# A four-layer decoder trunk: sums, additions and swaps issued in another order

## The chip, the cores and the metric

The kernel runs on one core of a Trainium2 chip. The metric is the device time of one execution in microseconds (us). TensorE (PE) multiplies matrices; VectorE (DVE), ScalarE (ACT) and GpSimd (POOL) work element by element; SyncE (SP) only issues transfers here, and ACT's queue issues some as well. Each engine runs its own list of instructions in order and waits on semaphores for the others.

## The reference, cut to what matters

There are four layers on 1032 tokens of 1024 features (1024 of a prompt, and 8 single tokens). Each layer adds a normed mixer to x:

```python
for i in range(DEPTH):
    kind, j = i % N_MIXERS, i // N_MIXERS          # a, b, c, a
    hp = rms_norm(xp, norm_pre[i])
    ...
    xp = xp + rms_norm(yp, norm_post[i])

def rms_norm(x, g):
    y = xf * lax.rsqrt(jnp.mean(xf * xf, axis=-1, keepdims=True) + NORM_EPS)
    return (y * g.astype(jnp.float32)).astype(x.dtype)
```

Mixer a is a gated MLP with a layer norm and a causal product inside chunks of 128 tokens; mixer b is attention over a window of 128 with rotary positions (each query is combined with its rotated, swapped halves); mixer c is a convolution of width 4, two gates by block-diagonal products, and a linear recurrence whose decay is

```python
log_a = -LRU_C * r.astype(jnp.float32) * jax.nn.softplus(-lam.astype(jnp.float32))
```

The softplus of `lam` depends on nothing but an input of 1024 numbers. The kernel calls it the decay constants.

## The kernel before, in words

Features lie on the partitions, tokens along the free axis, in three chunks of 344. A factor of a product is split in a high and a low part, and a product is three matmuls: high by high, high by low, low by high. One output tile of 128 features (a unit) so takes 8 x 3 x 3 = 72 matmuls of 128x344, and needs a weight block of 512 KB. SP loads these blocks (`weights(u)`, L422) into a ring of three; ACT makes the high part (`w_high`, L992), DVE the low part (`w_lo`, L1434), each for unit u while PE works on an earlier one. PE's second and first PSUM slots hold the result of a unit, and `evac` says that a slot is read.

A norm's mean of squares is a sum over partitions, made on PE by a product with `ones`. For the norm behind a mixer, `post(L, c)` (L605, L606) adds up for chunk c what DVE has summed in `ssq` and what ACT has squared last in `rx`. For the norm ahead of the next mixer, `square_sum` (L648) sums the squares of four feature tiles at a time, ACT copies the result (`copy_sums`, L1029), and `spread_sum` (L655) sums and spreads the copy to all partitions. The roots are taken on ACT as the exponential of a logarithm (L1017, L1019), `root_post` and `root_pre`.

At a border of two layers the order is written out by hand. PE runs `last_triple`: the last three output units of the old layer (j = 0, 1, 2), cut in nine pieces of one chunk each, with `post` for chunks 0 and 1 in between:

```python
TRIPLE = ((0, 0), (1, 0), (2, 0), (0, 1), (0, 2), (1, 1), (2, 1), (1, 2), (2, 2))
```

Then comes `first_pair` (L634): the first two units of the new layer, chunk by chunk. In chunk 0, all eight feature tiles of unit 0 and then of unit 1; in chunks 1 and 2, both units tile by tile. `post(prev, 2)` stands behind tile 3 of chunk 0, `spread_sum(c - 1)` behind tile 2 of chunk c. Meanwhile `cross` on ACT and on DVE turns the old result into the new x and the new operand. On ACT `out_squares` squares (L1008) and copies (L1010) each piece, and `tiles` makes the high part of x times gain (L1043) and the square (L1048). On DVE `out_add` adds the first half's part of the piece (layers a), `out_sum` adds a square to `ssq` (L1452), `tiles` multiplies two accumulator tiles by the root (L1473), makes the new x (L1476) and the low part (L1459), and `first_reads` (L1493) takes the results of the first two units out of PSUM. `next_weight(j)` copies the weights of the new layer's unit j. In a layer a three tiles of x are lent to other data (`A_EARLY`), and are fetched back per chunk by a DMA on ACT's queue (`x_own`, L1012).

In layer b the rotary combination needs each of eight query tiles with its quarters swapped. That is four DMAs a tile (L1228, `q_swap`), issued from ACT's queue when DVE has read the unit. In layer c the decay constants are a chain of 26 small DVE operations (L1918 to L1940) behind the sixth convolution tile.

At the start SP loads the first weight, pieces of x for chunk 0 and the second weight; ACT issues six small loads, loads its table and copies the first weight.

Of the kernel before, what the change touches and what calls it, by code (L numbers as in the profile page):

```python
# [17 lines left out]
ALU = mybir.AluOpType  # L18
# [67 lines left out]
def build(nc, io):  # L86
    with ExitStack() as ctx:
# [40 lines left out]
        zero = keep("zero", [P, 8])  # L128
# [18 lines left out]
        w_hi_done, w_lo_done = sem("w_hi_done"), sem("w_lo_done")  # L147
        result = sem("result")
# [15 lines left out]
        for i, kind in enumerate("abca"):  # L164
# [98 lines left out]
            if kind == "c":  # L263
# [35 lines left out]
                L.sp = at(n + "sp", o, [P, 6, KT]); o += 192  # L299
# [116 lines left out]
        def _(sp):  # L416
# [8 lines left out]
            weights(0)  # L425

# [4 lines left out]
            x_load(0, 0)  # L431
# [4 lines left out]
            for c in (1, 2):  # L436
                for g in range(X_PARTS[c]):
                    x_load(c, g)

# [25 lines left out]

            u = 2
# [76 lines left out]
        def _(pe):  # L543
# [64 lines left out]
            def last_triple(L, hi, lo):  # L608
# [10 lines left out]
                for j, c in TRIPLE:  # L619
# [3 lines left out]
                    if (j, c) == (2, 1):  # L623
                        post(L, 1)

            def first_pair(L, prev):
# [30 lines left out]
                pe.wait_ge(w_lo_done, u + 1)  # L657
                for c in range(CH):
# [3 lines left out]
                    if c == 0:  # L662
                        for k in range(KT):
                            pe.wait_ge(*L.hi_done.at(k + 1))
                            mm = products(0, k, 0)
# [3 lines left out]
                            if k == 3 and prev is not None:  # L669
                                post(prev, 2)  # L670
# [3 lines left out]
                        mm.then_inc(result, 1)  # L674
                    else:
                        for k in range(KT):
# [6 lines left out]
                            if k == 2:  # L683
                                spread_sum(c - 1)
# [295 lines left out]
        def _(act):  # L980
            act.dma_start(g_pre[:], io["g_pre"]).then_inc(gains, 16)
            act.dma_start(ident[:, :], io["ident"]).then_inc(consts, 16)
            act.dma_start(g_post[:], io["g_post"]).then_inc(consts, 16)
            act.dma_start(ln_g[:], io["ln_g"]).then_inc(consts, 16)
            act.dma_start(ln_b[:], io["ln_b"]).then_inc(consts, 16)
            act.dma_start(cvec[:], io["cvec"]).then_inc(consts, 16)
# [7 lines left out]
            def cross(prev, L):  # L994

                def out_squares(j, c):

                    slot = triple_slot(j)
                    if prev.kind == "a":
                        act.wait_ge(*prev.acc_done.at(LAST + TRIPLE.index((j, c)) + 1))  # L1000
# [10 lines left out]
                    elif j == 2:  # L1011
                        act.dma_start(x[:, 2:2 + A_EARLY, part(c)], prev.saved.rearrange("k p n -> p k n")[:, 2:2 + A_EARLY, part(c)]  # L1012
                                      ).then_inc(x_own[c], 16)
# [208 lines left out]
            def layer_b(L):  # L1222
# [20 lines left out]
                def unit_end(j):  # L1243
# [934 lines left out]
```

## Time and profile before

| what | value |
|---|---|
| time, median of three runs | 2393.58 us (2392.2 to 2395.04) |
| profiled execution | 2394.26 us, its span 2392.1 us |
| PE busy | 2320.3 us, 97% of the span, 15487 matmuls |
| DVE, ACT, POOL busy | 52%, 37%, 4% |
| high part of a weight block on ACT (L992) | 182 of 1.05 us |
| low part of a weight block on DVE (L1434) | 182 of 1.25 us |
| chain of work that ended last | PE 82%, DVE 9%, ACT 3% |

The span is the stretch from the first to the last instruction of the profile; the execution around it is 2.2 us longer. PE's 2320 us of work are one stream, and the rest of the span is the holes in it, the first 7.6 us ahead of its first matmul, and the last 15 us behind its last one. A wait is printed in brackets: how long the engine had been idle, and which instruction released it. The granted clock of a stretch is a share of 2.4 GHz.

### The profile page before, as it was taken

To read this page: it belongs to the slowest core of one execution; us is meant where nothing else is said; L and a number is where in the kernel's file an instruction comes from. 1 tells how busy PE (TensorE), PEld (TensorE's weight loads), DVE (VectorE), ACT (ScalarE), POOL (GpSimd) and SP (SyncE) were. 2 spreads that over 40 slices of the span, in tenths; PEclk is the share of its full clock that TensorE was granted. 3 is DMA by queue.
4 is the path that set the end of the run, shared out by engine and by line. 5 is a ranking of instruction groups with operands and counts; after the bars stand their busy time and mean duration, and the time that the engine had idled before them with its cause. 6 is when DMAs were issued, how large, how long until landed. Compare 5 with 4: busy or idle time off the path is not lost.

```text
span 2392.1 us, 36016 instructions
## 1 busy us (share of the span) xinstructions
PE 2320.3 (97%) x15487; PEld 2236.2 (93%) x15487; DVE 1232.4 (52%) x1759; ACT 889.1 (37%) x1280; POOL 90.7 (4%) x44
## 2 busy tenths in 40 slices
PE   8999999999999899998999999999999999999997
PEld 7999999999999798877989999979999999999996
DVE  4444445454433756667267888274444544545235
ACT  5323332332332534556352366363223332333221
POOL 0000000000000002222000010000000000000000
PEclk9999999999999999999999999999999999999998
DMA  4111111111121331111322111322111111111213
GB/s 137 45 45 45 45 45 38 43 45 45 36 98 45 127 111 54 45 45 37 107 83 70 45 45 45 118 84 77 45 54 36 45 45 38 43 45 45 89 46 107
DMA packets 58494, 145.86 MB, mean 61 GB/s; under 512 B 8904, under 2 KB 29528, under 8 KB 58328
## 3 DMA queue, kind: packets, MB, share of 16 engines
q1 hardware_dynamic: 53056, 135.34, 17.5%
q10 hardware_dynamic: 5280, 8.22, 1.3%
q8 instruction: 122, 2.00, 0.4%
q14 instruction: 36, 0.29, 0.0%
HBM read 121.47 MB, written 18.37 MB: 58 GB/s over the span
## 4 chain that ended last, share of the span: by engine, by line
PE 82%; DVE 9%; ACT 3%; DVEq 3%; ACTq 1%; issue 1%; DMA 1%; SPq 0%
PE ps L552 62%; PE ps L576 7%; PE ps L798 4%; PE ps L710 2%; PE ps L634 2%; DVE x L1476 1%; DVE l_acc L1473 1%; PE ps L816 1%; DVE w_lo L1434 1%; PE ps L855 1%; PE ps L844 1%; PE ps L703 1%; DVE l_sc L1773 1%; ACT l_h_hi L1043 1%; DVE l_hs L1988 1%
## 5 line engine op out<-in xcount | busy, mean ns | idle before, releaser
L552 PE MATMUL ps<-l_h_hi,w_hi 128*128 128x344 f32 x2448 | 527.1, 324 | 5.6 <-DVE w_lo L1434 5.6
L552 PE MATMUL ps<-l_h_lo,w_hi 128*128 128x344 f32 x2448 | 520.4, 321 | 0.0
L552 PE MATMUL ps<-l_h_hi,w_lo 128*128 128x344 f32 x2448 | 516.6, 319 | 0.0
L552 PEld LDWEIGHTS ps<-l_h_hi,w_hi 128*128 128x128 f32 x2448 | 409.2, 188 | 10.1 <-DVE w_lo L1434 6.8
L552 PEld LDWEIGHTS ps<-l_h_lo,w_hi 128*128 128x128 f32 x2448 | 414.7, 189 | 0.0
L552 PEld LDWEIGHTS ps<-l_h_hi,w_lo 128*128 128x128 f32 x2448 | 408.2, 188 | 0.0
L1434 DVE TENSOR_TENSOR w_lo<-w_raw,w_hi 128x1024 fp32r<-128x1024 f32 x182 | 227.7, 1252 | 250.3 <-ACT w_hi L992 240.2
L992 ACT ACTIVATE w_hi<-w_raw 128x1024 fp32r<-128x1024 f32 x182 | 190.8, 1049 | 109.9 <-DMA w_raw<-in_wu 78.9
L1551 DVE TENSOR_TENSOR l_tmp<-ps,rx 128x1032 f32<-128x1032 f32 x64 | 78.9, 1233 | 285.5 <-PE ps L552 285.3
L552 PE MATMUL ps<-l_y_lo,w_hi 128*128 128x344 f32 x816 | 173.1, 320 | 0.0
L552 PE MATMUL ps<-l_y_hi,w_hi 128*128 128x344 f32 x726 | 154.7, 321 | 0.8 <-DVEq L2002 0.8
L552 PE MATMUL ps<-l_y_hi,w_lo 128*128 128x344 f32 x726 | 153.1, 319 | 0.0
L1137 ACT ACTIVATE l_tmp<-l_tmp 128x1032 f32<-128x1032 f32 x32 | 34.2, 1067 | 303.9 <-DVEq L1592 303.9
L552 PEld LDWEIGHTS ps<-l_y_lo,w_hi 128*128 128x128 f32 x816 | 137.9, 189 | 0.0
L552 PEld LDWEIGHTS ps<-l_y_hi,w_hi 128*128 128x128 f32 x726 | 121.6, 188 | 1.7 <-DVEq L2002 1.1
L552 PEld LDWEIGHTS ps<-l_y_hi,w_lo 128*128 128x128 f32 x726 | 120.9, 188 | 0.0
L1142 ACT ACTIVATE l_tmp<-l_tmp 128x1032 f32<-128x1032 f32 x32 | 34.2, 1068 | 226.6 <-DVEq L1597 226.5
L1121 ACT ACTIVATE l_v<-l_v 128x1032 f32<-128x1032 f32 x32 | 34.1, 1067 | 214.9 <-DVEq L1573 214.9
L527 POOL TENSOR_TENSOR l_sc<-l_sc,l_rq 128x1024 f32<-128x1024 f32 x32 | 70.5, 2202 | 1072.6 <-DVE l_rq L1786 1072.6
L798 PE MATMUL ps<-l_h_hi,w_hi 128*128 128x344 f32 x288 | 97.1, 337 | 0.0
L1551 DVE TENSOR_TENSOR l_v<-ps,rx 128x1032 f32<-128x1032 f32 x28 | 34.5, 1233 | 120.2 <-PE ps L552 118.1
L1278 ACT ACTIVATE l_sc<-l_sc,l_mx 128x256 f32<-128x256 f32 x128 | 63.5, 497 | 82.3 <-DVEq L1779 82.3
(248 smaller groups left out, 3617.5 us busy)
## 6 DMA issues: line engine op xcount, KB each, us to landing
w_raw<-in_wu SPq DMA_DIRECT2D x182, 512.0 KB, 3.5
x_save<-x SPq DMA_DIRECT2D x9, 1376.0 KB, 5.8
x<-x_save SPq DMA_DIRECT2D x21, 516.0 KB, 7.1
l_sw<-l_q ACTq DMA_DIRECT2D x32, 129.0 KB, 2.8
out_y<-x SPq DMA_DIRECT2D x6, 688.0 KB, 3.5
x<-in_xt SPq DMA_DIRECT2D x4, 688.0 KB, 10.7
x<-in_xt SPq DMA_DIRECT2D x5, 516.0 KB, 6.7
x<-in_xt ACTq DMA_DIRECT2D x3, 516.0 KB, 3.6
```

Source lines behind the costliest of these rows:

```text
L527: nc.gpsimd.tensor_tensor(L.sc[:, i % 2], L.sc[:, i % 2], L.rq[:, i % 2].rearrange("p (h o) -> p h o", o=1).to_broadcast([P, 4, 2 * WIN]), ...
L552: mm = nc.tensor.matmul(ps[:, 3 * slot + ch, 0:CW], wt[:, w, k, :], mv[:, k, ch * CW:(ch + 1) * CW], start=(k == 0 and t == 0), stop=(k == ...
L576: mm = nc.tensor.matmul(ps[:, 3 * slot + ch, 0:CW], wt[:, u % W_RING, k, :], mv[:, k, part(ch)], start=(k == 0 and t == 0), stop=(k == KT ...
L634: mm = nc.tensor.matmul(ps[:, 3 * j + c, 0:CW], wt[:, (u + j) % W_RING, k, :], mv[:, k, part(c)], start=(k == 0 and t == 0), stop=(k == KT ...
L710: mm = nc.tensor.matmul(ps[:, 6 + b // 4, (b % 4) * P:(b % 4 + 1) * P], vt[:, b, :], L.ws[:, g, :], start=True, stop=True)
L798: mm = nc.tensor.matmul(ps[:, p % 2, 0:CW], wt[:, w % W_RING, k, :], mv[:, k, part(ch)], start=(k == 0 and t == 0), stop=(k == KT - 1 and ...
L992: nc.scalar.activation(w_hi[:, u % W_RING], w_raw[:, u % W_RING], ACT.Copy).then_inc(w_hi_done, 1)
L1137: nc.scalar.activation(L.tmp[:, 0, :], L.tmp[:, 0, :], ACT.Gelu_apprx_tanh).then_inc(L.u_act.sem, 1)
L1142: nc.scalar.activation(L.tmp[:, 1, :], L.tmp[:, 1, :], ACT.Silu).then_inc(L.g_act.sem, 1)
L1278: nc.scalar.activation(L.sc[:, p, h, :], L.sc[:, p, h, :], ACT.Exp, bias=L.mx[:, p, 1, h:h + 1], accum_out=L.mx[:, p, 2, h:h + 1])
L1434: V.tensor_tensor(w_lo[:, u % W_RING], w_raw[:, u % W_RING], w_hi[:, u % W_RING], ALU.subtract).then_inc(w_lo_done, 1)
L1551: V.tensor_tensor(chunks(out), psum_result(slot), chunks(rx[:]), ALU.mult)
```

## The change

It has five parts.

1. On PE `post(L, 1)` stands behind piece (1, 2) instead of (2, 1); `post(prev, 2)` and `spread_sum(0)` stand behind all of chunk 0, and `spread_sum(1)` behind tile 3 of chunk 2. ACT and DVE get a matching order: `next_weight(1)` ahead of the squares of the last pieces, `copy_sums(0)` inside chunk 1, `copy_sums(1)` behind two tiles of chunk 2 instead of six, `first_reads(0)` behind all of chunk 2. The fetch of lent x tiles is issued as soon as PE's result is there, and DVE waits for it at tile 2 instead of tile 0.
2. In layer b six of eight `q_swap` go from ACT's queue to SP's, each behind the weight load of a later unit.
3. The decay constants are computed in layer b's output units, in a buffer of their own, which stands in the place of an unused buffer of zeros.
4. The first weight is loaded and copied in halves of four feature tiles; x's first part is loaded between them.
5. Five small constant loads go from ACT's queue to SP's, behind x; ACT loads its table right behind its one remaining load.

```diff
@@ last_triple, first_pair (PE)
                     if (j, c) == (0, 1):
                         post(L, 0)
-                    if (j, c) == (2, 1):
+                    if (j, c) == (1, 2):
                         post(L, 1)
...
                             square_sum(k, 0)
-                            if k == 3 and prev is not None:
-                                post(prev, 2)
                         pe.wait_ge(w_lo_done, u + 2)
                         for k in range(KT):
                             mm = products(1, k, 0)
                         mm.then_inc(result, 1)
+                        if prev is not None:
+                            post(prev, 2)
+                        spread_sum(0)
...
                             square_sum(k, c)
-                            if k == 2:
-                                spread_sum(c - 1)
+                            if c == 2 and k == 3:
+                                spread_sum(1)
@@ cross (ACT)
+                        if j == 2:
+                            act.wait_ge(result, triple_done(prev, j, c))
+                            act.dma_start(x[:, 2:2 + A_EARLY, part(c)], prev.saved.rearrange("k p n -> p k n")[:, 2:2 + A_EARLY, part(c)]
+                                          ).then_inc(x_own[c], 16)
                         act.wait_ge(*prev.acc_done.at(LAST + TRIPLE.index((j, c)) + 1))
...
                     h_tiles(1, range(0, 1))
+                    next_weight(1)
                     out_squares(1, 2)
-                    h_tiles(1, range(1, 3))
+                    h_tiles(1, range(1, 2))
                     out_squares(2, 2)
-                    next_weight(1)
-                    h_tiles(1, range(3, 7))
+                    h_tiles(1, range(2, 4))
+                    if L is not None:
+                        copy_sums(0)
+                    h_tiles(1, range(4, 6))
                     root_post(2)
+                    h_tiles(1, range(6, 7))
...
                     w_high(L.u0 + 2)
+                    tiles(1, range(7, KT))
+                    root_pre(0)
                     tiles(2, range(0, 2))
-                    root_pre(0)
-                    tiles(2, range(2, 6))
                     copy_sums(1)
-                    tiles(2, range(6, KT))
+                    tiles(2, range(2, KT))
                     root_pre(1)
@@ cross (DVE)
-                                if prev.kind == "a":
-                                    dve.wait_ge(x_own[c], 16 * (prev.j + 1))
+                            if k == 2 and prev.kind == "a":
+                                dve.wait_ge(x_own[c], 16 * (prev.j + 1))
...
                     tiles(1, range(0, 2))
                     out_add(1, 2)
+                    next_weight(1)
                     out_sum(1, 2)
+                    out_add(2, 2)
                     tiles(1, range(2, 4))
-                    out_add(2, 2)
-                    next_weight(1)
                 tiles(1, range(0 if prev is None else 4, KT))
                 if L is not None:
                     w_low(L.u0 + 2)
-                tiles(2, range(0, 2))
+                tiles(2, range(KT))
                 if L is not None:
                     first_reads(0)
-                tiles(2, range(2, KT))
@@ layer b: swaps (SP), decay constants (DVE)
+                sp.wait_ge(*L.in_done.at(j + 1))
+                sp.wait_ge(*L.rotated.at(m))
+                for a in range(4):
+                    b = a ^ 1
+                    sp.dma_start(L.sw[32 * a:32 * a + 32, :], L.q[32 * b:32 * b + 32, m, :]).then_inc(L.sw_done.sem, 16)
...
                 while u < L.u1:
                     weights(u)
+                    if L.kind == "b" and 9 <= u - L.u0 <= 18:
+                        is_q, m = piece_tile(3 * (u - L.u0 - 9))
+                        if is_q:
+                            q_swap(L, u - L.u0 - 3, m)
...
-                    if is_q:
-                        q_swap(j, m)
-                    elif m % 2:
+                    if not is_q and m % 2:
...
+                    if L.kind == "b" and m == 1:
+                        decay_constants(layers[2])
...
-                    if m == 5:
-                        decay_constants()
@@ start (ACT)
-            act.dma_start(ident[:, :], io["ident"]).then_inc(consts, 16)
...
+            nc.scalar.preload_act_table_set("natural_log_exp_and_others")
...
-                    w_high(0)
+                    act.wait_ge(w_first, 16)
+                    nc.scalar.activation(w_hi[:, 0, 0:4], w_raw[:, 0, 0:4], ACT.Copy).then_inc(w_first_high, 1)
                     tiles(0, range(0, 2))
+                    act.wait_ge(w_loaded[0], 16)
+                    nc.scalar.activation(w_hi[:, 0, 4:8], w_raw[:, 0, 4:8], ACT.Copy).then_inc(w_hi_done, 1)
+                    tiles(0, range(2, 4))
                     w_high(1)
-                    tiles(0, range(2, KT))
+                    tiles(0, range(4, KT))
```

How the order moves, at three places. PE in `first_pair` from a to b, chunk 0, before, where `ssq` and `rx` are the inputs of `post(prev, 2)`:

```order
L634 MATMUL ps<-l_h_hi,w_lo 128x344
L634 MATMUL ps<-l_h_lo,w_hi 128x344
L648 MATMUL ps<-l_squares,ones 32x344 x4
L605 MATMUL ps<-ssq,ones 128x344
L606 MATMUL ps<-rx,ones 128x344
L634 MATMUL ps<-l_h_hi,w_hi 128x344
L634 MATMUL ps<-l_h_hi,w_lo 128x344
```

PE at the end of the same chunk 0 now; its four square sums are further up, and `rx` is also what `spread_sum(0)` (L677) reads:

```order
L656 MATMUL ps<-l_h_hi,w_hi 128x344
L656 MATMUL ps<-l_h_hi,w_lo 128x344
L656 MATMUL ps<-l_h_lo,w_hi 128x344
L627 MATMUL ps<-ssq,ones 128x344
L628 MATMUL ps<-rx,ones 128x344
L677 MATMUL ps<-rx,ones 128x344
L656 MATMUL ps<-l_h_hi,w_hi 128x344
L656 MATMUL ps<-l_h_hi,w_lo 128x344
```

The sum for chunk 2 moved from the middle of chunk 0 to its end, and the spreading sum follows at once.

ACT in `cross` from a to b, chunk 2, before; L1017 and L1019 are the root of chunk 0, L1029 the copy of chunk 1's square sums:

```order
L1017 ACTIVATE rx<-ps,eps 128x344
L1019 ACTIVATE rx<-rx 128x344
L1043 ACTIVATE l_h_hi<-x,g_pre 128x344
L1048 ACTIVATE l_squares<-x 128x344
L1043 ACTIVATE l_h_hi<-x,g_pre 128x344
L1048 ACTIVATE l_squares<-x 128x344
L1043 ACTIVATE l_h_hi<-x,g_pre 128x344
L1048 ACTIVATE l_squares<-x 128x344
L1043 ACTIVATE l_h_hi<-x,g_pre 128x344
L1048 ACTIVATE l_squares<-x 128x344
L1029 ACTIVATE rx<-ps 128x344
L1043 ACTIVATE l_h_hi<-x,g_pre 128x344
```

The same place now, with L1042 and L1044 the root and L1054 the copy:

```order
L1042 ACTIVATE rx<-ps,eps 128x344
L1044 ACTIVATE rx<-rx 128x344
L1068 ACTIVATE l_h_hi<-x,g_pre 128x344
L1073 ACTIVATE l_squares<-x 128x344
L1068 ACTIVATE l_h_hi<-x,g_pre 128x344
L1073 ACTIVATE l_squares<-x 128x344
L1054 ACTIVATE rx<-ps 128x344
L1068 ACTIVATE l_h_hi<-x,g_pre 128x344
```

Before, tiles 0 and 1 of chunk 2 stand ahead of the root, and tiles 2 to 5 between root and copy. Now tiles 0 and 1 stand between them, so the copy has two tiles of chunk 2 ahead of it instead of six.

SP's queue in layer b, before, where `w_raw<-in_wu` is a weight load:

```order
L496 DMA out_ks<-in_kct 128x1016
L497 DMA out_vs<-in_vct 8x16256
L422 DMA w_raw<-in_wu 128x1024 x3
L509 DMA out_vp<-l_vtok 128x128
L510 DMA out_vs<-l_v_104 8x128
L422 DMA w_raw<-in_wu 128x1024 x10
L500 DMA l_kc<-in_kcb 128x8x128
```

SP's queue now, in the stretch of the second of the two rows of weight loads:

```order
L423 DMA w_raw<-in_wu 128x1024
L482 DMA l_sw<-l_q 32x1032 x4
L423 DMA w_raw<-in_wu 128x1024
L482 DMA l_sw<-l_q 32x1032 x4
L423 DMA w_raw<-in_wu 128x1024 x3
L482 DMA l_sw<-l_q 32x1032 x4
L423 DMA w_raw<-in_wu 128x1024
L482 DMA l_sw<-l_q 32x1032 x4
L423 DMA w_raw<-in_wu 128x1024 x3
L482 DMA l_sw<-l_q 32x1032 x4
L423 DMA w_raw<-in_wu 128x1024
L482 DMA l_sw<-l_q 32x1032 x4
```

Six of the ten loads now have four swap transfers behind them.

## Rows read from the trace of the kernel before

**Rows 1.** PE's waits, whole span: line, releaser, us in total, times, longest us
```profile
PE ps L605 <- ACT rx L1008: 12.9, 5, 4.4
PE ps L844 <- ACT l_pt L1287: 10.5, 7, 3.2
PE ps L655 <- ACT rx L1029: 8.5, 3, 2.9
PE ps L816 <- DVEq L1779: 7.9, 4, 2.8
...
PE ps L552 <- DVE w_lo L1434: 5.6, 4, 3.1
```

**Rows 2.** PE's timeline: start, us, instruction, count [idle before, releaser]
```profile
791.18 0.53 PE L605 MATMUL ps<-ssq,ones 128*128 128x344 f32 x1 [4.40 <-ACT rx L1008]
...
827.80 0.56 PE L655 MATMUL ps<-rx,ones 128*128 128x344 f32 x1 [2.77 <-ACT rx L1029]
...
1226.40 0.53 PE L605 MATMUL ps<-ssq,ones 128*128 128x344 f32 x1 [2.71 <-ACT rx L1008]
...
1261.58 0.56 PE L655 MATMUL ps<-rx,ones 128*128 128x344 f32 x1 [2.85 <-ACT rx L1029]
```

**Rows 3.** Stretch behind 791.18: busy us per engine, granted clock, DMA share, GB/s
```profile
790.00:800.00 10.00, 8.82 (x43) 8.19 (x44) 7.70 (x14) 5.66 (x12) 0.00 (x0) 0.83 0.27 76
```

**Rows 4.** ACT's timeline, border b to c
```profile
1225.83 0.44 ACT L1008 ACTIVATE rx<-ps 128x344 f32<-128x344 f32 x1
...
1261.10 0.44 ACT L1029 ACTIVATE rx<-ps 128x344 f32<-128x344 f32 x1
```

**Rows 5.** PE's timeline, border b to c: chunk 2 starts
```profile
1255.57 0.43 PE L634 MATMUL ps<-l_h_hi,w_hi 128*128 128x344 f32 x1
...
1258.41 0.32 PE L634 MATMUL ps<-l_h_lo,w_hi 128*128 128x344 f32 x1
```

**Rows 6.** DVE's timeline, border b to c: chunk 2
```profile
1249.55 0.87 DVE L1473 TENSOR_TENSOR l_acc<-l_acc,rx 128x688 f32<-128x688 f32 x1
...
1254.81 0.87 DVE L1473 TENSOR_TENSOR l_acc<-l_acc,rx 128x688 f32<-128x688 f32 x1
...
1257.70 0.86 DVE L1473 TENSOR_TENSOR l_acc<-l_acc,rx 128x688 f32<-128x688 f32 x1
```

**Rows 7.** Timeline in layer b: ACT's queue issuing, and PE
```profile
896.63 2.44 ACTq L1228 DMA_DIRECT2D l_sw<-l_q  x4
...
901.14 0.44 PE L844 MATMUL ps<-l_pt,l_vtok 128*64 128x256 f32 x2 [1.50 <-ACT l_pt L1287]
...
1066.05 0.69 PE L844 MATMUL ps<-l_pt,l_vtok 128*64 128x256 f32 x2 [3.20 <-ACT l_pt L1287]
```

**Rows 8.** Timeline in layer c: DVE, and PE
```profile
1341.72 0.17 DVE L1918 TENSOR_SCALAR l_sp<-l_sp 128x8 f32<-128x8 f32 x1
...
1346.43 2.25 DVE L1930 TENSOR_SCALAR l_sp<-l_sp 128x8 f32<-128x8 f32 x1
...
1352.29 2.41 DVE L1966 SCALAR_TENSOR_TENSOR l_xc<-l_st,cvec,l_xc 128x8 f32<-128x8 f32 x1
...
1364.95 0.42 PE L552 MATMUL ps<-l_h_hi,w_hi 128*128 128x344 f32 x1 [3.06 <-DVE w_lo L1434]
```

**Rows 9.** Stretch of layer b's output units, columns as in rows 3
```profile
1146.00:1196.00 50.00, 50.00 (x321) 49.54 (x318) 11.51 (x12) 13.79 (x14) 0.00 (x0) 1.00 0.36 127
```

**Rows 10.** Timeline of the start: ACT, and PE
```profile
3.79 1.28 ACT L1050 ACT_TABLE_LOAD   x1 [3.79 <-issue]
...
7.57 0.62 PE L634 MATMUL ps<-l_h_hi,w_hi 128*128 128x344 f32 x1 [7.57 <-DVE w_lo L1434]
```

**Rows 11.** DVE's timeline at the end of the last layer
```profile
2380.51 0.87 DVE L1473 TENSOR_TENSOR l_acc<-l_acc,rx 128x688 f32<-128x688 f32 x1 [1.05 <-DMA x<-x_save]
```

**Rows 12.** SP's queue in layer b: loads of weights
```profile
935.09 0.33 SPq L422 DMA_DIRECT2D w_raw<-in_wu  x1
...
952.14 0.33 SPq L422 DMA_DIRECT2D w_raw<-in_wu  x1
```

More of the change, by code:

```diff
@@ L429, in x_load @@
                 sp.dma_start(x[:, ks, part(c)], io["xt"].rearrange("k p n -> p k n")[:, ks, part(c)]).then_inc(x_in[c][g], 16)
-            x_load(0, 0)
+            for half in range(2):
+                ks = slice(4 * half, 4 * half + 4)
+                sp.dma_start(w_raw[:, 0, ks], io["wu"][0].rearrange("p (k m) -> p k m", m=P)[:, ks]
+                             ).then_inc(w_first if half == 0 else w_loaded[0], 16)
+                if half == 0:
+                    x_load(0, 0)
             x_load(0, 1)
@@ L664, in first_pair @@
                             pe.wait_ge(*L.hi_done.at(k + 1))
+                            if prev is None and k == 4:
+                                pe.wait_ge(w_lo_done, 1)
                             mm = products(0, k, 0)
@@ L1495, in cross @@
                 if prev is None:
-                    w_low(0)
+                    dve.wait_ge(w_first_high, 1)
+                    V.tensor_tensor(w_lo[:, 0, 0:4], w_raw[:, 0, 0:4], w_hi[:, 0, 0:4], ALU.subtract).then_inc(w_first_low, 1)
                     tiles(0, range(0, 2))
+                    dve.wait_ge(w_hi_done, 1)
+                    V.tensor_tensor(w_lo[:, 0, 4:8], w_raw[:, 0, 4:8], w_hi[:, 0, 4:8], ALU.subtract).then_inc(w_lo_done, 1)
+                    tiles(0, range(2, 4))
                     w_low(1)
-                    tiles(0, range(2, KT))
+                    tiles(0, range(4, KT))
                 else:
@@ L1514, in cross @@
                     out_add(0, 2)
+                    tiles(0, range(2, 4))
                     out_sum(0, 2)
-                    tiles(0, range(2, 4))
                     out_add(1, 1)
+                    tiles(0, range(4, 6))
                     out_sum(1, 1)
-                    tiles(0, range(4, 6))
+                    out_add(2, 1)
                     next_weight(0)
-                    out_add(2, 1)
                     tiles(0, range(6, KT))
@@ L1552, in read, with decay_constants @@
                 V.drain().then_inc(evac[slot], 3)
+            def decay_constants(L):
+                dve.wait_ge(*L.sp_e.at(1))
+                V.tensor_scalar(L.sp[:, 2], L.sp[:, 0], 2.0, None, ALU.add)
+                V.drain()
+                V.reciprocal(L.sp[:, 2], L.sp[:, 2])
+                V.drain()
+                V.tensor_tensor(L.sp[:, 2], L.sp[:, 2], L.sp[:, 0], ALU.mult)
+                V.drain()
+                V.tensor_tensor(L.sp[:, 3], L.sp[:, 2], L.sp[:, 2], ALU.mult)
+                V.memset(L.sp[:, 4], 1.0 / 17)
+                V.drain()
+                for d in (15, 13, 11, 9, 7, 5, 3, 1):
+                    V.tensor_tensor(L.sp[:, 4], L.sp[:, 4], L.sp[:, 3], ALU.mult)
+                    V.drain()
+                    V.tensor_scalar(L.sp[:, 4], L.sp[:, 4], 1.0 / d, None, ALU.add)
+                    V.drain()
+                V.tensor_tensor(L.sp[:, 4], L.sp[:, 4], L.sp[:, 2], ALU.mult)
+                V.tensor_scalar(L.sp[:, 5], cvec[:, 7], -1.0, 0.0, ALU.mult, ALU.max)
+                V.drain()
+                V.tensor_scalar(L.sp[:, 4], L.sp[:, 4], 16.0, None, ALU.mult)
+                V.drain()
+                V.scalar_tensor_tensor(L.sp[:, 1], L.sp[:, 5], 8.0, L.sp[:, 4], ALU.mult, ALU.add)
+                V.drain()
+                V.tensor_scalar(L.sp[:, 2], L.sp[:, 1], -1.0, None, ALU.mult)
+                V.drain().then_inc(L.sp_done.sem, 1)
             def yssq(L):
```

71 lines of the change are left out of this document (24 added, 47 removed).

## The prediction

> **What bounds the kernel now.** One core runs, and the time is the length of TensorE's (PE's) instruction stream with its holes. So the first view to read is the list of what PE waited for [rows 1], then the timeline at the longest of these waits. The list has five lines that matter: the roots' sums of the layer borders (L605, 12.9 us; L655, 8.5 us), attention (L844, 10.5 us; L816, 7.9 us) and the products of layer c (L552, 5.6 us). Work that ends sooner on another engine is worth something only where it shortens one of these holes.
>
> At a border PE runs the last three output units of one layer and the first two units of the next. Two holes come back there [rows 2]. The sum that spreads chunk 1's squares of the output (post(1), L605) starts 4.40 us late from a to b and 2.71 us late from b to c; c to a repeats the second at 1575.45 with 2.71. The sum of the next norm's squares (spread(1), L655) is 2.77 and 2.85 us late, and c to a repeats 2.85 at 1610.65. Behind one of the two PE drops to half speed for a few us: the stretch 790 to 800 has a granted clock of 0.83 [rows 3], so 10 x 0.17 = 1.7 us of work are lost, and the stretches from 1262 and from 1611 read 0.83 as well.
>
> **The borders.** Both holes have one shape: PE asks for the result of a step whose input it has only just made. Piece (2,1) ends at 1226.40 - 2.71 = 1223.7; its square runs on ACT from 1225.83 for 0.44 us, and PE starts the sum at 1226.40 [rows 2, 4]. The change puts piece (1,2) between. One tile of PE work for two units is 6 matmuls; three such tiles took 1255.57 to 1258.41 for 17 steps, or 0.167 us a matmul with the start, 0.157 in a run [rows 5]. A piece of 24 matmuls is 3.8 us, so the new post(1) comes up at 1223.7 + 3.8 = 1227.5, 1.2 us after the square ended. The 2.71 us hole goes; chunk 1's root comes 1.1 us later than before. From a to b the hole is 4.40 us, of which 3.8 are covered by the piece and the rest by the weight copy and square that ACT now does in another order. I take the whole hole.
>
> Spread(1) waited for the copy at 1261.10 [rows 4], which ACT did behind six tiles of chunk 2. The change has it behind two. It needs PE's last square sum of chunk 1, at about 1252.5 in the new order, so it is done by 1253.0. PE asks for it only behind tile k = 3 of chunk 2, 4 x 0.94 + 0.9 = 4.7 us after that. The hole goes too.
>
> What is late next is DVE in chunk 2. It starts two tiles every 2.9 us (1254.81 to 1257.70, [rows 6]), 1.45 us a tile, where PE needs 0.94. In the trace chunk 2 began at 1249.55 on DVE and 1255.57 on PE. PE now gets there sooner by the 2.71 us and a restart, at 1252.7. DVE comes sooner too, since the weight copy of unit u0+2 is placed ahead of tile (1,7) and the early read of chunk 0 behind all tiles: about 1247.9. The low part of tile 3 is then ready at 1247.9 + 2 x 2.9 + 2.0 = 1255.7, and PE wants it at 1252.7 + 3 x 0.94 + 0.3 = 1255.8. The square sums (0.9) and spread(1) (0.6) give DVE time behind that, so tile 7 is level again. I charge 0.3 us of wait at each border. The load of unit u0+1 is issued at the end of piece (1,2) as before; its copies on ACT and DVE are moved ahead of squares and sums by less than 2 us, and PE wants them only behind eight tiles of chunk 0.
>
> Sum: a to b 4.40 + 2.77 + 1.7 + 0.3 (two restarts of PE) = 9.2 us. b to c 2.71 + 2.85 + 1.7 + 0.3 - 0.3 = 7.3, c to a the same with a little less waiting, 7.6. Together **24.1 us**. Bounds: 0.5 x 24 where DVE takes back half of it, 25 where nothing is late.
>
> **Swaps on the weights' queue.** In layer b four DMA issues hold ACT for 2.44 us [rows 7], before the weight copy and the copy of the transposed scores, and PE waits 1.50 us behind it at 901.14 and 3.20 us at 1066.05; a third place, 998.19, reads 1.46 behind an issue of 3.19 us. The swaps at 919.58, 970.75 and 1040.52 have no wait of PE behind them: worth nothing. At 901.14 the next wait, 1.53 us at 912.38 for DVE, may grow, so I take 1.2; at 998.19 1.5; at 1066.05 no more than the issue gives, 2.4. Sum **5.1 us**, bounds 0 (DVE takes all of it back) and 6.2.
>
> **Decay constants.** DVE works on them from 1341.72 to 1349.8, 8.1 us in the convolutions of layer c; w_lo is copied behind them, and PE waits 3.06 us for it at 1364.95 [rows 8]. From there waits of 0.8 to 1.2 us repeat on L955 and L552 until 1498.03 while DVE never rests, so a shorter DVE chain is worth its length, until PE's waits (5.6 + 1.2 + 0.8 + 0.7 = 8.3 us) are used up. One tiny operation of 128x8 took 2.25 us at 1346.43, as GpSimd (POOL) multiplied beside it; the same happened to another at 1352.29, 2.41 us. POOL's start is set by ACT and PE, which don't move, so 2.1 us of the 8.1 pass on to whatever DVE does then: **6.0 us**. Bounds 3.1 (the first wait alone) and 8.1. In their new place, behind layer b's output units, DVE was busy 11.5 of 50 us and POOL not at all [rows 9]; 6 us more there are covered by the unit of 11.35 us. If that cover were gone they would cost their 6 us.
>
> The Trainium skill ("SBUF — State Buffer", Who interferes with whom) has DVE and GpSimd share a port pair that one instruction holds to its end while the other fully blocks. By that rule the sum is the 6.0 us. By a reading in which the stall belonged to the tiny operation it would be 8.1 us. The trace agrees with the rule at 1346.43 and 1352.29.
>
> **Start.** ACT's table load begins at 3.79 and ends at 5.07, behind six DMA issues; now it is behind one. The first weight is copied in halves, which saves half of 1.06 us on ACT and of 1.23 us on DVE. PE starts at 7.57 [rows 10]. The first matmul comes between 7.57 - 1.1 = 6.5 (the data land as late as ACT was ready) and 3.9 (they are there 2.6 us sooner). The loads are still under way then, so I take 5.9, or 1.7 us, and 0.3 for two short waits behind it: **2.0 us**, bounds 0 and 2.9.
>
> **End.** No next layer takes the time. DVE starts chunk 2 at 2380.51 after 1.05 us of wait for x [rows 11] and works to the end. The early DMA removes that wait; chunk 1's root, now 1.7 us later, gives most of it back: **0.3 us**, bounds -1 and 1.5.
>
> **Sum.** 24.1 + 5.1 + 6.0 + 2.0 + 0.3 = 37.5 us. The profiled execution took 2394.26 (span 2392.1), so 2356.8; the median is 0.7 lower: 2356.
>
> **Rivals.**
> - DVE sets chunk 2. If it can't start before 1249.55, PE waits 1.7 us more at tile 3, loses about as much again at tile 5, and the clock may fall again. Half of the borders' 24 us goes: 2368. For: the margin is 0.1 us. Against: w_lo, ahead of it, waited 1.1 us for ACT.
> - Borders as forecast, but layers b and c give only their certain parts (2.4 and 3.1): 2362.
> - More is won: layer c 8.1, start 2.9, attention 6.2 and no wait in chunk 2: 2351.
> - Slower: SP's queue. Each of six swaps waits on SP for the read of unit j and a rotation on DVE, and every later weight load is queued behind it. Loads are issued 17 us apart (935.09, 952.14) [rows 12], two units ahead of use, so about 28 us may pass before PE sees it. Beyond 28 + 6 us of holding at each of six swaps the kernel is slower. Held for 37 us, it loses 6 x 9 = 54 us against 37.5 won: 2410. Against: the load just before the swap waits for PE's end of the same unit.
> - The edits don't do it: the waits reappear unchanged one step later, as ACT and DVE set the borders all along: 2392.
>
> **How the numbers follow.** Forecast 2356 (its own range 2352 to 2361) 52%; DVE-bound borders 20%; smaller b and c 12%; more won 10%; no change 3%; slower 3%. The range that leaves out less than 2 in 10 is 2348 to 2369. A difference of 0.2% (4.8 us) is about what a measurement of this kernel can tell from no change. Faster by over that: 0.94; within: 0.03; slower: 0.03.
>
> **What would show it.** In the new trace the three inner borders have no wait over 0.5 us for post(1) and spread(1), and the stretches behind read a clock near 1; a wait on the low parts in chunk 2 speaks for the first rival. In layer b, waits on the copy of transposed scores fall by 5 us; a wait on w_hi or w_lo with SP's queue held names the slower rival. In layer c the first wait of 3.06 is gone. The first matmul is near 5.9. Wrong would be a new wait at the borders' weights, or the chain of layer c bound by PE's gate results.

## The result, and the profile after

The changed kernel takes 2358.41 us (median of four runs, 2357.96 to 2358.68) where the kernel before took 2392.89 us beside it (2392.04 to 2395.04). The ratio is 0.9855, with a 95% interval of 0.9844 to 0.9867. The profiled execution took 2358.17 us, its span 2356.3 us. It lies 2.4 us above the forecast of 2356 and inside the forecast's own range.

PE's waits in the changed kernel, in the form of [rows 1]. L627 is now the sum post (L605 before), L677 the spreading sum (L655), L844 and L872 are attention, its scores and its transposed scores (L816 and L844), L574 is L552, L983 is L955, and L656 is the first pair (L634). Its 5.6 us on ACT is the time up to the first matmul of all:

```profile
PE ps L844 <- DVEq L1842: 10.2, 6, 2.8
PE ps L656 <- ACT l_h_hi L1068: 5.6, 1, 5.6
PE ps L872 <- ACT l_pt L1321: 5.0, 4, 2.6
PE ps L574 <- DVE w_lo L1465: 2.8, 4, 0.9
PE ps L627 <- ACT rx L1036: 2.4, 1, 2.4
PE ps L656 <- DVE l_h_lo L1490: 1.4, 4, 0.7
PE ps L574 <- DVEq L2037: 0.8, 1, 0.8
PE ps L983 <- ACTq L1384: 0.8, 3, 0.3
```

The wait on L677 is no longer in the list, and the only wait left on L627, 2.4 us, is that of post(2) at the very end. Waits of layer b on DVE (L844) have grown from 7.9 to 10.2 us, while those on the transposed scores (L872) fell from 10.5 to 5.0. Layer c's waits for `w_lo` are at 0.9 us at most; the 3.06 of [rows 8] is gone.

The stretch behind the a to b border, against [rows 3]:

```profile
790.00:800.00 10.00, 10.00 (x70) 8.46 (x70) 8.32 (x15) 5.97 (x13) 0.00 (x0) 1.00 0.72 226
```

PE's granted clock is 1.00 there, after 0.83, and PE is busy all of the 10 us.

Five rows of the border b to c, against [rows 2, 5, 6]: post(1), the start of chunk 2 on DVE and on PE, the one wait in it, and spread(1):

```profile
1211.18 0.74 PE L627 MATMUL ps<-ssq,ones 128*128 128x344 f32 x2
...
1231.89 0.87 DVE L1504 TENSOR_TENSOR l_acc<-l_acc,rx 128x688 f32<-128x688 f32 x1
...
1236.49 0.42 PE L656 MATMUL ps<-l_h_hi,w_hi 128*128 128x344 f32 x1
...
1240.15 0.43 PE L656 MATMUL ps<-l_h_lo,w_hi 128*128 128x344 f32 x1 [0.24 <-DVE l_h_lo L1490]
...
1241.70 0.56 PE L677 MATMUL ps<-rx,ones 128*128 128x344 f32 x1
```

Neither sum has a wait. DVE starts chunk 2 at 1231.89, 4.6 us ahead of PE's 1236.49; the forecast had 4.8. PE waits 0.24 us at tile 3, where 0.3 was charged.

To see where the time went, the two traces are cut at places that both have: the start of post(0) at a border, and the first matmul behind the spreading sum of chunk 2, inside the new layer's third unit. The lengths compare so:

| stretch | before, us | after, us | less | forecast |
|---|---|---|---|---|
| start and first layer a, to post(0) | 774.12 | 770.81 | 3.31 | 2.0 |
| border a to b | 65.00 | 56.25 | 8.75 | 9.2 |
| layer b | 371.95 | 367.87 | 4.08 | 5.1 |
| border b to c | 63.34 | 56.22 | 7.12 | 7.3 |
| layer c | 285.70 | 279.79 | 5.91 | 6.0 |
| border c to a | 63.42 | 56.22 | 7.20 | 7.6 |
| second layer a, to post(0) | 727.81 | 728.28 | -0.47 | 0 |
| end, to the last instruction | 40.76 | 40.86 | -0.10 | 0.3 |
| sum | 2392.1 | 2356.3 | 35.8 | 37.5 |

### The profile page after: what moved, and what is told of

Read it like the earlier page. It is cut to its first block, busy times and chain, and to the rows that moved or that the text cites. A ratio compares the mean times of both kernels' runs of the same rounds, so it can differ in the third digit from the quotient of the medians.

```text
span 2356.3 us, 36020 instructions
## 1 busy us (share of the span) xinstructions
PE 2311.0 (98%) x15487; PEld 2230.4 (95%) x15487; DVE 1232.3 (52%) x1759; ACT 888.8 (38%) x1281; POOL 91.5 (4%) x44
## 4 chain that ended last, share of the span: by engine, by line
PE 86%; DVE 7%; DVEq 2%; ACT 2%; ACTq 1%; issue 1%; DMA 1%; SPq 0%
PE ps L574 63%; PE ps L598 8%; PE ps L826 5%; PE ps L738 2%; PE ps L656 2%; PE ps L844 1%; PE ps L883 1%; PE ps L731 1%; PE ps L872 1%; DVE l_sc L1836 1%; DVE w_lo L1465 1%; DVE x L1507 1%; DVE l_hs L2023 1%; DVE l_acc L1504 1%; PE ps L858 1%
## 5 line engine op out<-in xcount | busy, mean ns | idle before, releaser
L574 PE MATMUL ps<-l_h_hi,w_hi 128*128 128x344 f32 x2448 | 526.6, 323 | 2.8 <-DVE w_lo L1465 2.8
L574 PE MATMUL ps<-l_h_lo,w_hi 128*128 128x344 f32 x2448 | 519.7, 320 | 0.0
L574 PE MATMUL ps<-l_h_hi,w_lo 128*128 128x344 f32 x2448 | 516.2, 319 | 0.0
L574 PEld LDWEIGHTS ps<-l_h_hi,w_hi 128*128 128x128 f32 x2448 | 408.9, 188 | 7.2 <-DVE w_lo L1465 4.0
L574 PEld LDWEIGHTS ps<-l_h_lo,w_hi 128*128 128x128 f32 x2448 | 414.0, 189 | 0.0
L574 PEld LDWEIGHTS ps<-l_h_hi,w_lo 128*128 128x128 f32 x2448 | 407.8, 188 | 0.0
L574 PE MATMUL ps<-l_y_lo,w_hi 128*128 128x344 f32 x816 | 173.2, 320 | 0.0
L574 PE MATMUL ps<-l_y_hi,w_hi 128*128 128x344 f32 x726 | 154.8, 321 | 0.8 <-DVEq L2037 0.8
L574 PE MATMUL ps<-l_y_hi,w_lo 128*128 128x344 f32 x726 | 153.1, 319 | 0.0
L574 PEld LDWEIGHTS ps<-l_y_lo,w_hi 128*128 128x128 f32 x816 | 137.9, 189 | 0.0
L574 PEld LDWEIGHTS ps<-l_y_hi,w_hi 128*128 128x128 f32 x726 | 121.6, 188 | 1.7 <-DVEq L2037 1.1
L574 PEld LDWEIGHTS ps<-l_y_hi,w_lo 128*128 128x128 f32 x726 | 120.9, 188 | 0.0
L1584 DVE TENSOR_TENSOR l_v<-ps,rx 128x1032 f32<-128x1032 f32 x28 | 34.5, 1233 | 119.6 <-PE ps L574 118.5
```

What stands on the lines that cost most here:

```text
L574: mm = nc.tensor.matmul(ps[:, 3 * slot + ch, 0:CW], wt[:, w, k, :], mv[:, k, ch * CW:(ch + 1) * CW], start=(k == 0 and t == 0), stop=(k == ...
L1584: V.tensor_tensor(chunks(out), psum_result(slot), chunks(rx[:]), ALU.mult)
```

## Each part alone

Four kernels each have one part of the change on top of the kernel before. They ran on one chip, where the kernel before had a median of 2391.92 us.

**The borders.** All edits of part 1 of the change, on PE, ACT and DVE, and nothing else:

```diff
-                    if (j, c) == (2, 1):
+                    if (j, c) == (1, 2):
                         post(L, 1)
...
-                            if k == 2:
-                                spread_sum(c - 1)
+                            if c == 2 and k == 3:
+                                spread_sum(1)
```

> Only the order at the borders (and the earlier fetch of lent x tiles) is added to the kernel before. My theory: the holes at post(1) and spread(1) and the half-speed stretches behind them go, 24 us (8.8, 7.1 and 7.2 at the three borders in the trace of the changed kernel, about 23), so about 2370 us. Rival, DVE sets chunk 2 and the parts of the change only help together: 12 us or less, 2381 or more.

Measured: 2370.34 us, ratio 0.9908 (0.9895 to 0.9922), 21.6 us less. The 50 us from about post(1) of a to b on, busy time of PE, PEld, DVE, ACT, POOL, then granted clock:

```profile
787.00:837.00 50.00, 49.77 (x318) 43.45 (x317) 35.76 (x60) 27.65 (x56) 0.00 (x0) 1.00 0.57 184
```

The gain stands by itself and is of the size of the traces' 23 us. The rival of 12 us is out.

The 23 us come from one pair of executions. In the traces of the three other kernels that keep the old borders (the swaps, the decay constants and the start alone), the three borders are together 20.8 to 22.0 us longer than in the changed kernel, about what was measured here. There spread(1) from b to c and from c to a waits 1.40 to 1.75 us and not the 2.85 of [rows 2]; the last section shows why.

**The swaps.** Six `q_swap` on SP's queue:

```diff
-                    if is_q:
-                        q_swap(j, m)
-                    elif m % 2:
+                    if not is_q and m % 2:
```

> Only the six swaps go from ACT's to SP's queue. My theory: 4 to 5 us less (4.1 us between the sums of squares that frame layer b in the two traces), about 2389 us; the waits for the copy of transposed scores fall from 10.5 to about 5 us. Rival, DVE sets attention and the 4 us come from elsewhere: no difference that can be told.

Measured: 2388.81 us, ratio 0.9983 (0.9974 to 0.9992), 3.1 us less, with an interval of 1.9 to 6.2: no difference is ruled out, 4 to 5 us is not. The two waits of attention in this kernel, here L828 for the scores and L856 for the transposed scores:

```profile
PE ps L828 <- DVEq L1789: 10.6, 6, 2.8
...
PE ps L856 <- ACT l_pt L1297: 5.5, 6, 2.5
```

Against the kernel before, the second fell from 10.5 to 5.5 us, as expected, and the first rose from 7.9 to 10.6. How the two share their sum varies: four kernels with the old swaps read 9.1 to 10.9 for the second and 7.9 to 9.8 for the first. Their sum is steadier, 18.4 to 18.9 us there and 16.1 here, 2.3 to 2.8 us less. So DVE takes back a part of what ACT gives, between a fifth and a half.

**The decay constants.**

```diff
                     V.drain().then_inc(L.yssq_done.sem, 1)
+                    if L.kind == "b" and m == 1:
+                        decay_constants(layers[2])
...
-                    if m == 5:
-                        decay_constants()
```

> Only the decay constants move to layer b's output units. My theory: DVE's chain in layer c is shorter by 8.1 us and meets both of POOL's products, so 6.0 us less, 2387 us. Rival, the stall of 2.25 us went with the tiny operation: 8.1 us less, 2385 us. Rival, only the first wait goes: 3.1 us.

Measured: 2386.65 us, ratio 0.9976 (0.9966 to 0.9985), 5.3 us less, with an interval of 3.6 to 8.1. That rules out the rival of 3.1 us; between 6.0 and 8.1 the trace has to decide. POOL's first product, the two DVE operations beside POOL's products, and the copy of `w_lo` for which PE had waited 3.06 us [rows 8]:

```profile
1345.86 3.32 POOL L534 TENSOR_TENSOR l_it<-l_it,l_xc 128x1032 f32<-128x1032 f32 x1 [202.64 <-ACTq L1368]
...
1346.82 2.38 DVE L1965 SCALAR_TENSOR_TENSOR l_xc<-l_st,cvec,l_xc 128x8 f32<-128x8 f32 x1
...
1351.81 2.40 DVE L1965 SCALAR_TENSOR_TENSOR l_xc<-l_st,cvec,l_xc 128x8 f32<-128x8 f32 x1
...
1357.37 1.22 DVE L1431 TENSOR_TENSOR w_lo<-w_raw,w_hi 128x1024 fp32r<-128x1024 f32 x1 [0.16 <-issue]
```

The stall is still there. It now falls on a 128x8 operation of the convolution, 2.38 us where others of its line take 0.22. The copy starts at 1357.37 instead of 1363.67, 6.3 us earlier; the weight copy ahead of the chain, at 1340.25 instead of 1340.58, was 0.3 us early already. That leaves 6.0 us, not 8.1. The Trainium skill ("SBUF — State Buffer", Who interferes with whom) says that where the two engines contend for the ports they share, the later one fully blocks until the other is done; the trace agrees, and it also shows the reverse, since POOL's product took 3.32 us here, where others of its line take 2.4 to 2.5, and began at 1345.86 while a 128x1024 operation of DVE ran from 1345.62 for 1.28 us.

**The start.**

```diff
+                    act.wait_ge(w_first, 16)
+                    nc.scalar.activation(w_hi[:, 0, 0:4], w_raw[:, 0, 0:4], ACT.Copy).then_inc(w_first_high, 1)
                     tiles(0, range(0, 2))
```

> Only the start is changed (first weight in halves, table load early, constants on SP's queue); the order of sums in the first pair is that of before. My theory: 2.0 us from the first matmul that comes 2 us sooner and 1.3 us from a shorter half-speed stretch, 3.3 us less, 2389.5 us. Rival, the 1.3 us came from the order of the sums in the first pair: 2.0 us less, and the half-speed stretch is as long as before.

Measured: 2389.14 us, ratio 0.9989 (0.998 to 0.9998), so 0.5 to 4.8 us less. Its first matmul, against [rows 10]:

```profile
5.45 0.63 PE L644 MATMUL ps<-l_h_hi,w_hi 128*128 128x344 f32 x1 [5.45 <-ACT l_h_hi L1054]
```

It comes 2.1 us sooner. From first matmul to first post(0), this trace has 764.74 us and the kernel before 766.55, so another 1.8 us came behind it. In the start-up PE's matmuls begin 0.286 us apart, and later 0.157. I call the first stretch slow. It ended at 17.1 in the kernel before and at 9.0 here. The first pair's order was that of before here, so the rival, which needs the new order, is out. How much of the 1.8 us belongs to the edit is less clear. Of the four kernels that start like the one before, three (17.1, 16.3 and 17.3) took 766.2 to 766.6 us from first matmul to post(0). The fourth, with the borders alone, ended its slow stretch at 14.0 and took 764.58, though its orders differ from those of the kernel before only later than that. So a part of it can vary from execution to execution. What ends the slow stretch was not settled.

The four gains, 21.6 + 3.1 + 5.3 + 2.8 = 32.8 us, make the change's 34.5 within their intervals. Nothing shows that the parts hinder each other.

## What removed the holes at the borders

The forecast gave each hole one cause. Each of these kernels is the changed one with something undone. The changed kernel ran again beside three of them, the one with post(1) back, the one with the late copy and the one with post(1) early in the last layer. The other four ran on another chip without it; there the kernel before took 2392.22 us, 1.6 less than beside this rerun, so differences of those four from 2357.95 can be too small by up to 1.6 us.

> The changed kernel once more, as the measure for the three others on the same chip: 2358 us, and a spread well below the 8 us of the kernel before, since the stretches at lower clock are gone.

Measured: 2357.95 us (2357.21 to 2358.21), the kernel before beside it 2393.79.

**post(1) back behind piece (2,1), on PE alone.**

```diff
-                    if (j, c) == (1, 2):
+                    if (j, c) == (2, 1):
                         post(L, 1)
```

> The changed kernel with one thing undone: PE asks for post(1) behind piece (2,1) again, ACT and DVE keep the new order. My theory: the hole of post(1) returns at the three inner borders, 4.4 + 2.7 + 2.7 us with some clock behind it, about 10 to 14 us in all, 2368 to 2372. In the last layer the sum comes sooner and the end gains up to 1.5. Rival, the other orders on ACT and DVE had removed the hole: 2358.

Measured: 2363.87 us, ratio 0.9875 (0.9861 to 0.989), 5.9 us more than the changed kernel, and well below the 10 to 14 of my theory. Post(1) from a to b, ACT's square ahead of post(1) from b to c, and that post(1):

```profile
785.87 0.53 PE L627 MATMUL ps<-ssq,ones 128*128 128x344 f32 x1 [2.32 <-ACT rx L1036]
...
1211.69 0.46 ACT L1036 ACTIVATE rx<-ps 128x344 f32<-128x344 f32 x1 [0.32 <-PE ps L598]
...
1212.29 0.53 PE L627 MATMUL ps<-ssq,ones 128*128 128x344 f32 x1 [0.64 <-ACT rx L1036]
```

The holes came back as 2.32 and 0.64 us, where [rows 2] have 4.40 and 2.71 (c to a repeats 0.64). In the kernel before, ACT's square began 2.1 us after the piece was done [rows 4], behind a pair of tiles for which ACT had waited on DVE:

```profile
1223.98 0.58 ACT L1043 ACTIVATE l_h_hi<-x,g_pre 128x344 fp32r<-128x344 f32 x1 [0.91 <-DVE x L1476]
```

Now ACT has its tiles done and waits 0.32 us for PE's piece. On DVE the change also has an edit that part 1 of its description leaves out: squares are added behind the next pair of tiles and not ahead of it.

```diff
                     out_add(0, 2)
+                    tiles(0, range(2, 4))
                     out_sum(0, 2)
-                    tiles(0, range(2, 4))
```

With it the tiles reach ACT sooner. So the new orders of ACT and DVE together took 2.1 us of each hole, and PE's piece in between covers the rest. Which of their edits does it was not run. From a to b the hole of 2.3 us cost 4.1 us in all (the border is 60.05 us instead of 55.93, both measured to the spreading sum of chunk 2). The rest is lower clock, 0.66 and 0.77 in the first two stretches of 3 us behind the hole. From b to c the hole of 0.64 us cost 0.9, and the clock read 1.00.

**The copy of chunk 1's sums back behind six tiles, on ACT alone.**

```diff
-                    tiles(2, range(0, 2))
+                    tiles(2, range(0, 6))
                     copy_sums(1)
-                    tiles(2, range(2, KT))
+                    tiles(2, range(6, KT))
```

> The changed kernel with ACT's copy of chunk 1's square sums behind six tiles of chunk 2 instead of two; PE still asks for it behind tile 3. DVE makes the tiles at 1.45 us each, so the copy comes 4 x 1.45 = 5.8 us later, where 4.7 us of PE's work were between. My theory: the wait at spread(1) returns with 1 to 3 us at each of three borders, and clock behind it: 2361 to 2370. Rival, PE's place of the sum alone had removed the wait: 2358.

Measured: 2356.59 us (2355.7 to 2359.76), ratio 0.9848 (0.9834 to 0.9863): not to be told from the changed kernel, and the rival was right. The only wait at the spreading sum in it:

```profile
PE ps L677 <- ACT rx L1054: 0.2, 1, 0.2
```

With PE's new place the early copy isn't needed, and it has a price. In the changed kernel ACT stands waiting for PE's last square sum of chunk 1, and DVE then waits for the high part behind it:

```profile
1236.63 0.46 ACT L1054 ACTIVATE rx<-ps 128x344 f32<-128x344 f32 x1 [1.37 <-PE ps L670]
...
1237.59 0.58 DVE L1490 SCALAR_TENSOR_TENSOR l_h_lo<-x,g_pre,l_h_hi 128x344 fp32r<-128x344 f32 x1 [0.54 <-ACT l_h_hi L1068]
```

These 0.54 us are why PE waits 0.24 us at tile 3: with the copy late that wait is gone at all three borders.

**PE's spread(1) back behind tile 2, with the late copy.**

```diff
-                            if c == 2 and k == 3:
+                            if c == 2 and k == 2:
                                 spread_sum(1)
```

> The changed kernel with both places of chunk 1's next sum as before: ACT's copy behind six tiles of chunk 2, PE's sum behind tile 2. The copy alone cost nothing. My theory now: PE's place is what counts; PE asks 0.94 + 0.9 = 1.8 us sooner, where the late copy left 0 to 0.2 us, so 1.8 us of wait come back at three borders with some clock, 5 to 8 us: 2363 to 2366. Rival, DVE's earlier start in chunk 2 had removed the wait: 2358.

Measured: 2364.97 us, ratio 0.9884 (0.9869 to 0.9899), 7.0 us more than the changed kernel's 2357.95. The wait:

```profile
PE ps L677 <- ACT rx L1054: 5.7, 3, 2.3
```

**The same, with DVE's early read of chunk 0 back as well.**

```diff
-                tiles(2, range(KT))
+                tiles(2, range(0, 2))
                 if L is not None:
                     first_reads(0)
+                tiles(2, range(2, KT))
```

> The same with DVE's early read of chunk 0 back as well, so that all of chunk 2 is as before and only the order ahead of it is new. If the three edits of chunk 2 are all that removed the 2.8 us waits at spread(1), these come back whole: 8.4 us and clock behind them, 2367 to 2370. If the order ahead of chunk 2 had its part in it, less comes back: 2361 to 2366.

Measured: 2369.28 us, ratio 0.9899 (0.9882 to 0.9915), 11 us more. The wait:

```profile
PE ps L677 <- ACT rx L1054: 8.0, 3, 2.8
```

It is 8.0 us, of the 8.5 in [rows 1]. So the edits of chunk 2 removed that hole, and not the order ahead of it. With the copy late, PE's place carries 5.5 us of it and DVE's read 2.3. Whether the early copy alone would do it, with PE's place as before, was not run.

**DVE's early read back alone.**

> The changed kernel with DVE's early read of chunk 0 back behind two tiles of chunk 2. It puts 0.94 us of DVE's work, and a wait for the root if there is one, ahead of tiles 2 to 7, where PE waits 0.24 to 0.7 us for low parts as it is. My theory (DVE is just level with PE in chunk 2): PE waits 0.9 to 1.5 us more at each of three borders, 3 to 5 us in all, 2361 to 2363. Rival, the square sums and the sum for chunk 1 give DVE time enough: 2358.

Measured: 2359.06 us, ratio 0.9861 (0.9846 to 0.9875), 1.1 us above the changed kernel, which is no clear difference. PE's wait for low parts, here of the three borders alone, where the changed kernel has 3 x 0.24 (its list counts 0.7 us of the start as well):

```profile
PE ps L656 <- DVE l_h_lo L1490: 1.6, 3, 0.7
```

My theory fell. 0.94 us of DVE's work in this place cost PE 0.2 to 0.5 us a border. The wait stays at one tile; PE's square sums and spread(1) follow right behind it, and they probably give DVE the rest of the time. DVE was not as near to setting chunk 2 as the forecast had it.

## The start and the end

**The first weight whole again**, with the early table load kept:

> The changed kernel with the first weight loaded and copied whole; ACT's table load and the constants' place stay new. My theory: the halves save the second half of ACT's and DVE's copy, 0.5 + 0.6 us, and the landing of 256 KB less; the first matmul comes at 6.7 to 7.3 instead of 5.4 to 5.8, 1 to 1.5 us more in all: 2359. Rival, x's first tiles and not the weight set the start: the same time, 2358.

Measured: 2361.57 us, ratio 0.9871 (0.9856 to 0.9885), 3.2 to 3.6 us more than the changed kernel and more than the 1 to 1.5 expected. The rival, that x sets the start, is out. In the trace all of it lies ahead of the first post(0), at 774.23 us where the changed kernel has 770.81. ACT's first copy and the first matmul:

```profile
4.89 1.06 ACT L1010 ACTIVATE w_hi<-w_raw 128x1024 fp32r<-128x1024 f32 x1 [2.43 <-DMA g_pre<-in_g_pre]
...
7.38 0.62 PE L652 MATMUL ps<-l_h_hi,w_hi 128*128 128x344 f32 x1 [7.38 <-DVE w_lo L1455]
```

The same in the changed kernel:

```profile
3.68 0.63 ACT L1081 ACTIVATE w_hi<-w_raw 128x512 fp32r<-128x512 f32 x1 [1.22 <-DMA g_pre<-in_g_pre]
...
5.58 0.63 PE L656 MATMUL ps<-l_h_hi,w_hi 128*128 128x344 f32 x1 [5.58 <-ACT l_h_hi L1068]
```

The early table load alone brings no more than 0.2 to 0.4 us (7.38, where the four kernels with the old start have 7.54 to 7.78), since ACT then waits until 4.89 for the transfer of `g_pre`. These 16 KB land 4.1 us behind their issue beside a weight load of 512 KB, and 2.9 us beside one of 256 KB, so that ACT begins at 3.68. Of the 1.8 us by which the first matmul comes sooner, 1.2 are this transfer. The halved copies, 0.63 us instead of 1.06 on ACT and 0.69 instead of 1.22 on DVE, are the smaller part.

**post(1) early in the last layer only.**

> The changed kernel, with post(1) behind piece (2,1) in the last layer only, where DVE's chain and not PE sets the end. DVE waited 3.3 us for chunk 1's root there. My theory: the root comes 2 to 3 us sooner, DVE then is busy without a hole to the end, 1.0 to 1.7 us less: 2357. Rival, the second root or PE's last piece sets the end: 2358.

Measured: 2357.78 us (2357.45 to 2359.9), ratio 0.985 (0.9834 to 0.9867): no difference. In the changed kernel DVE waits for chunk 1's root:

```profile
2334.22 0.88 DVE L1504 TENSOR_TENSOR l_acc<-l_acc,rx 128x688 f32<-128x688 f32 x1 [3.33 <-ACT rx L1044]
```

With post(1) early that wait is 1.14 us, but another took its place:

```profile
2333.31 0.88 DVE L1504 TENSOR_TENSOR l_acc<-l_acc,rx 128x688 f32<-128x688 f32 x1 [1.14 <-ACT rx L1044]
...
2339.71 0.52 DVE L1476 TENSOR_TENSOR l_acc<-ps,l_acc 128x344 f32<-128x344 f32 x1 [2.05 <-PE ps L598]
```

PE, held up by post(1), ends its last piece later, and DVE's last addition waits 2.05 us for it. The rival was right. No version ran that is clearly faster than the changed kernel.

## Why the prediction was right

- **Borders, 24.1 us forecast, 23.1 measured.** The size was right, the working in part not. The piece of 24 matmuls, 3.8 us, is longer than a hole of 2.71, but it had less left to cover: 2.1 us of each hole were removed by the orders on ACT and DVE, which the forecast named only from a to b. The step in which the copy has two tiles ahead of it instead of six, so that the hole at spread(1) goes too, named a cause that was not needed: PE's place of the sum, 1.8 us of its work later, and DVE's earlier tiles remove the hole with the copy late as well.
- **The sum of the borders.** It takes 0.3 us of wait off from b to c and next to nothing at the other two, though the text charges it at each; the wait of 0.24 came at all three. It also counts 2.85 us of hole and 1.7 of lost clock from b to c and from c to a, as one execution had them, where three others of the same order were 1.1 to 1.5 us shorter at each of these borders. By the medians of the borders alone the term is 21.6 us and not 24.1. That is the size of the whole miss, 2356 forecast and 2358.41 measured, and it is in part luck that the errors of the other terms, between -1.0 and +1.3 us, largely cancel.
- **DVE level with PE in chunk 2.** The lead (4.8 forecast, 4.6 measured) and the wait (0.3, 0.24) were right. The rival built on a margin of 0.1 us was given 20%, which was too much: 0.94 us of extra work at each border moved the time by about 1 us in all.
- **Layer b, 5.1 forecast, 4.1 measured.** The waits behind the first two swaps went as taken. The mis-sized term is the third, 2.4 us, "no more than the issue gives". The wait of 3.20 us of [rows 7] is gone, but waits follow behind it. The issues of one of the six swaps, and these waits:

```profile
906.88 2.48 SPq L482 DMA_DIRECT2D l_sw<-l_q  x4
...
1062.04 0.49 PE L844 MATMUL ps<-l_kd,l_q 64*128 64x256 f32 x2 [1.34 <-DVEq L1842]
...
1066.43 0.44 PE L872 MATMUL ps<-l_pt,l_vtok 128*64 128x256 f32 x2 [0.67 <-ACT l_pt L1321]
```

The four issues take SP 2.48 us, and no engine waits behind them. The 1.34 us for the scores is new, and the 0.67 for the transposed scores was 0.27 in the kernel before (at 1082.33 there): 1.7 of the 3.2 us come back, and 1.5 are won where 2.4 were taken. The total of 4.1 is itself uncertain. Nine traces of the changed layer b spread over 2.9 us, four of the old one over 0.8, with stretches at lower clock between the waits; their means are 4.1 us apart.
- **Layer c, 6.0 forecast, 5.9 measured.** The stall of 2.1 us passed on, here in the changed kernel's own trace, and the chain's waits are now 0.9 us:

```profile
1322.94 3.32 POOL L556 TENSOR_TENSOR l_it<-l_it,l_xc 128x1032 f32<-128x1032 f32 x1 [196.92 <-ACTq L1402]
...
1323.90 2.38 DVE L2001 SCALAR_TENSOR_TENSOR l_xc<-l_st,cvec,l_xc 128x8 f32<-128x8 f32 x1
...
1363.07 0.42 PE L574 MATMUL ps<-l_h_hi,w_hi 128*128 128x344 f32 x1 [0.89 <-DVE w_lo L1465]
```

- **Start, 2.0 forecast, 3.3 measured.** The first matmul came at 5.58 where 5.9 was taken. The missing term is the slow stretch behind it, which ended sooner, 1.3 us of the 3.3.
- **End, 0.3 forecast, -0.1 measured.** Chunk 1's root, later, gives back what the early transfer won, and with an early root PE's last piece does. The second layer a lost 0.5 us that was not forecast. It did so, by 0.2 to 0.5 us, in every kernel with ACT's early copy and in none without it, and a wait of 0.18 us for a weight's low part stands at its beginning; the rest was not traced.
- **The slower rival.** SP's queue: the loads of weights behind the swaps are issued as far apart as they were, 17 to 22 us, and 44 us at the last swap where it had been 48. PE never waits on a weight in layer b.

## What to carry to other kernels

Where an engine asks for a result that it has only just fed, put work that is ready between the two; but look first at what holds the result up on the engine that makes it, since an order there may give a part of it for nothing. Where two edits are aimed at one wait, it is removed only once: undo them one by one before giving either the credit. And a stall from two engines at one port belongs to the pair, not to the instruction on which it shows: here 8.1 us of instructions were taken away, the stall of 2.1 us fell on the next one, and 6.0 us were won.

## What the runs showed of the hardware

A hole of 2.7 us in PE's work costs more than its length in one execution and not in the next. Behind post(1) from b to c, after the same hole of 2.71 us, the first 3 us read a granted clock of 1.00 in the kernel before and of 0.59 in the kernel with the decay constants alone:

```profile
1226.40:1229.40 3.00, 3.00 (x16) 2.60 (x17) 2.93 (x6) 1.58 (x4) 0.00 (x0) 1.00 0.00 0
...
1227.49:1230.49 3.00, 3.00 (x8) 2.22 (x9) 2.92 (x6) 1.57 (x4) 0.00 (x0) 0.59 0.00 0
```

The four kernels with the old borders have this hole twice each, from b to c and from c to a. Behind six of the eight holes the clock fell, behind two, both in the kernel before, it did not. Where it fell, PE came later to spread(1), found a hole of 1.40 to 1.75 us there, and kept its full clock behind that one. Where it did not fall, the hole at spread(1) was 2.85 us and the clock fell behind it. So the profile before shows one of two courses, and the other is 1.1 to 1.5 us shorter at each of these borders. From a to b, with the same holes of 4.40 and 2.77 us, 50 us read a clock of 0.97 in the kernel before and of 0.93 in the kernel with the start alone, where it fell twice:

```profile
785.00:835.00 50.00, 44.98 (x267) 37.65 (x268) 33.99 (x57) 25.56 (x54) 0.00 (x0) 0.93 0.43 144
```

The kernel before varies from 2389.43 to 2397.17 us in 25 runs on one chip. The changed kernel, whose borders read 1.00, stays within 2357.21 to 2358.68 in the eight runs of the same code. That the holes make the spread is not shown. The kernel with the decay constants alone keeps them all and spreads over 2.6 us in nine runs, while the one with the late copy, with one hole of 0.2 us at its borders, spreads over 4.1 us in four.

At the start PE's matmuls of 128x344 began 0.286 us apart for 3.5 to 9.5 us behind the first one. That is the spacing of stretches with a granted clock of 0.50, as at 793 in the kernel before, but here the profile reads 1.00.
